# A decoder layer with 32 experts: a fourth load slot, filler products, routing spread over engines, and a write-then-add of the expert sums

## What is computed

```python
logits = (hf @ w_router + b_router).astype(jnp.float32)
top_val, top_idx = lax.top_k(logits, TOP_K)            # TOP_K = 4
gate = jax.nn.softmax(top_val, axis=-1)
...
down = lax.ragged_dot(clamped_swiglu(up), w_down, group_sizes) + b_down[e_sorted]
out = jnp.zeros_like(hf).at[tok].add(down * g_sorted[:, None].astype(down.dtype))
```

## Time and profile before

| what | value |
|---|---|
| time, median of 3 (lowest, highest) | 1441.86 us (1438.42 to 1442.68) |
| the profiled execution's own time | 1445.39 us |
| its span | 1442.3 us |
| TensorE busy | 1299.9 us (90%) |
| VectorE, ScalarE, GpSimd busy | 626.7, 341.7, 313.1 us |
| mean granted clock | 0.978 |
| DMA | 483.70 MB, mean 335 GB/s |

### The profile page before, as it was taken

One profiled execution on the slowest core, in us unless ns is written; L12 is line 12 of the kernel. 1 busy time (PEld: TensorE's weight loads), 2 busy tenths in 40 slices (PEclk: granted clock), 3 DMA queues, 4 the chain that ended last, 5 costly groups with the idle time before them and its releaser, 6 DMA issues.

```text
span 1442.3 us, 45649 instructions
## 1 busy us (share of the span) xinstructions
PE 1299.9 (90%) x18586; PEld 764.2 (53%) x18587; DVE 626.7 (43%) x1667; ACT 341.7 (24%) x860; POOL 313.1 (22%) x423
## 2 busy tenths in 40 slices
PE   5999999999988998988989977899999999998992
PEld 2454555665545555554545534455555555555551
DVE  2467455885573433323333323234334333333335
ACT  2111014774321222211212211122222222221221
POOL 0300002554002222221222211122222222221221
PEclk9999999999999999999999989999999999999996
DMA  9658504003789999999999999999979899999995
GB/s 353 231 206 291 179 12 175 2 2 126 299 334 397 367 396 418 423 427 423 412 423 405 399 425 426 423 418 412 414 322 421 356 370 400 421 425 424 414 419 226
DMA packets 65775, 483.70 MB, mean 335 GB/s; under 512 B 9660, under 2 KB 16612, under 8 KB 45000
## 3 DMA queue, kind: packets, MB, share of 16 engines
q1 hardware_dynamic: 57312, 465.36, 78.0%
q0 software_dynamic: 8144, 17.78, 4.7%
q10 hardware_dynamic: 280, 0.02, 0.0%
HBM read 467.58 MB, written 19.93 MB: 338 GB/s over the span
## 4 chain that ended last, share of the span: by engine, by line
PE 64%; DMA 27%; DVE 5%; issue 2%; ACT 0%; SPq 0%; DVEq 0%; POOL 0%; POOLq 0%; ACTq 0%
PE ps L1953 25%; DMA arena<-in_w_down 23%; PE ps L1973 15%; PE ps L1604 7%; PE ps L1854 4%; PE ps L1719 2%; PE ps L1751 2%; PE ps L1785 2%; DMA arena<-in_w_ada 1%; PE ps L1571 1%; PE ps L1961 1%; DMA arena<-token_numbers 1%; DVE arena L996 1%; DMA arena<-in_w_in 1%; PE ps L1527 1%
## 5 line engine op out<-in xcount | busy, mean ns | idle before, releaser
L1953 PE MATMUL ps<-arena 128*32 128x256 f32 x10240 | 586.8, 383 | 45.6 <-issue 29.4
L1953 PEld LDWEIGHTS ps<-arena 128*32 128x32 f32 x10240 | 343.2, 111 | 266.3 <-issue 57.2
L1973 PE MATMUL ps<-arena 128*32 128x256 f32 x5120 | 302.4, 386 | 40.5 <-DMA arena<-in_w_down 36.2
L1446 DVE TENSOR_SCALAR arena<-ps 128x128 f32<-128x128 f32 x160 | 46.4, 290 | 570.8 <-PE ps L1961 566.2
L1973 PEld LDWEIGHTS ps<-arena 128*32 128x32 f32 x5120 | 155.7, 110 | 164.0 <-issue 45.5
L918 ACT ACTIVATE arena<-ps,arena 32x256 f32<-32x256 f32 x316 | 147.3, 466 | 359.6 <-DMA token_sums<-arena 218.3
L678 POOL DMA_INDIRECT arena<-xn_rows,arena x82 | 85.5, 1043 | 421.9 <-DVE arena L1414 269.3
L670 POOL DMA_INDIRECT token_sums<-arena x80 | 110.4, 1380 | 219.7 <-ACT arena L918 216.7
L909 ACT ACTIVATE arena<-arena 128x128 f32<-128x128 f32 x160 | 49.5, 310 | 416.5 <-DVE arena L1446 416.5
L1604 PE MATMUL ps<-arena 128*128 128x512 f32 (+1 forms) x320 | 129.7, 561 | 2.9 <-DMA arena<-in_w_in 2.9
L653 POOL TENSOR_SCALAR arena<-arena 128x128 f32<-128x128 f32 (+3 forms) x48 | 51.7, 1083 | 204.8 <-DVE arena L1213 193.0
(11 more groups left out here) (339 smaller groups left out, 980.7 us busy)
## 6 DMA issues: line engine op xcount, KB each, us to landing
arena<-in_w_up SPq DMA_DIRECT2D x68, 2048.0 KB, 10.6
arena<-in_w_down SPq DMA_DIRECT2D x64, 2048.0 KB
arena<-in_w_up SPq DMA_DIRECT2D x30, 4096.0 KB
arena<-in_w_ada SPq DMA_DIRECT2D x12, 2048.0 KB, 11.0
arena<-in_w_in SPq DMA_DIRECT2D x5, 2048.0 KB, 9.6
arena<-in_w_o SPq DMA_DIRECT2D x2, 2048.0 KB, 10.9
arena<-in_x SPq DMA_DIRECT2D x4, 512.0 KB, 5.2
arena<-in_w_cmp_v SPq DMA_DIRECT2D x2, 1024.0 KB, 12.5
```

What stands on the lines that cost most here:

```text
L1953: ins = pe.matmul(out_of(y, g), xgT[:, 2 * n + k, :], tiles[par][n][:, k, at:at + 256], start=(n == 0 and k == 0), stop=False)
L1973: ins = pe.matmul(out_of(5, g), actT[:, y, k, :], tiles[par][4 + y][:, k, 256 * g:256 * (g + 1)], start=False, stop=(y == 1 and k == 3))
```

## The change

1. **A fourth load slot.** `ring` gets a fourth buffer. "ada" 8 and 10 go there, and "in" 4 is issued right after "ada" 8, into slot 1, ahead of "ada" 9. The first half of the other compression weight (`wv_half[0]`) and the clearing of `blk`, whose memory the slot overlaps, wait until the row of "ada" 10 is done.
2. **Filler products** of 128 columns: nine before the first modulation product, six before the second, two before tiles 4 and 5 are turned.
3. **Routing.** The gates are normalized before the places are known; GpSimd splits them into three parts and puts a sign on them; the table scaled by token numbers is that of slots (512 columns) and no longer that of chunks (1664); ScalarE copies `picked` and writes `gidx_all`; the gate tables follow after the first rows' transpose. `gate_bits`, `picked` and `tok_chunk` leave the memory of one weight tile, whose load waits no longer for the gates.
4. **Sums.** The sign of a gate tells whether the pair is in the lowest chunk of its token. From it two lists of rows are made. Each chunk issues two scatters: one that writes the rows of tokens met for the first time, one that adds the others. Either list has the other's rows out of bounds. Whoever waited for the one landing waits for both.
5. The last tile's x2 rows are stored after its normed rows.

```diff
-        ring = [take(8192, 4096), take(12288, 4096), take(20480, 4096)]
+        ring = [take(8192, 4096), take(12288, 4096), take(20480, 4096), take(28672, 4096)]
...
-                (("ada", 8), 1), (("ada", 9), 0), (("ada", 10), 1), (("ada", 11), 0), (("in", 4), 1), (("c1", 0), 2),
+                (("ada", 8), 3), (("in", 4), 1), (("ada", 9), 0), (("ada", 10), 3), (("ada", 11), 0), (("c1", 0), 2),
...
-                if (kind, m) == ("ada", 9):
+                if (kind, m) == ("ada", 11):
                     sp.wait_ge(bias_out, 96)
+                    sp.wait_ge(row_sb, ADA_AT[10] + 1)
                     sp.dma_start(wv_half[0], w_c1[1][:, 0:8, :]).then_inc(wv_in, 16)
...
+            idle_products(9)
             pe.wait_ge(silu_ready, 1)
...
             turn_tiles(range(4))
+            idle_products(6)
             ada(2)
             ada_t(0)
             ada_t(2)
+            idle_products(2)
             turn_tiles((4, 5))
...
             def add_rows(c):
                 pool.wait_ge(written, c * 16 + FILLED)
+                pool.wait_ge(placed, c * 16 + FILLED)
                 pool.sem_inc(turn, 1)
+                pool.tensor_copy(idxw, row_first[:, bass.ds(c, 1)]).then_inc(row_idx_moved, 1)
                 pool.tensor_copy(idxs, row_all[:, bass.ds(c, 1)]).then_inc(row_idx_moved, 1)
...
                 pool.wait_ge(y_ready, c + 2)
                 pool.sem_inc(turn, 1)
+                pool.indirect_dma_start(acc_d, bass.IndirectOffsetOnAxis(idxw, 0), ybuf, None,
+                                        bounds_check=SEQ - 1, oob_is_err=False).then_inc(placed, 16)
                 scatter(acc_d, ybuf)
...
             with act_e.Fori(0, total - 1) as c:
                 act_e.wait_ge(tile_used[5], c + 1)
                 act_e.wait_ge(written, c * 16 + FILLED)
+                act_e.wait_ge(placed, c * 16 + FILLED)
...
+            act_e.activation(picked, ps[0:32, 3, 0:NT * MAX_CH].rearrange("p (i c) -> p i c", c=MAX_CH), ACT.Copy)\
+                .then_inc(picked_sb, 1)
+            act_e.wait_ge(spread_ps, 1)
+            act_e.activation(gidx_all, ps[:, 2, 0:MAX_CH], ACT.Identity, scale=-1.0, bias=ck[:, C_QUART:C_QUART + 1])\
+                .then_inc(idx_ready, 1)
...
-            v.tensor_scalar(tok_chunk, in_chunk, const(C_TOK, 1), None, ALU.mult).then_inc(pick_ready, 1)
+            v.tensor_scalar(in_slot_tok, in_slot, const(C_TOK, 1), None, ALU.mult).then_inc(pick_ready, 1)
```

More of the change, by code:

```diff
@@ L206, in hybrid_layer @@
         row_all = take(cur[0] + 8 * MAX_CH, MAX_CH, parts=SLOTS, dt=I32)
+        row_first = take(cur[0], MAX_CH, parts=SLOTS, dt=I32)
+        row_no, first_mark = [take(cur[0] + n * MAX_CH, MAX_CH, parts=SLOTS) for n in (1, 2)]
+        gate_bits = take(cur[0] + 9 * MAX_CH, 24).bitcast(BF16).rearrange("p (m n) -> p m n", n=16)
         ybuf = put(D)[SLOTS:2 * SLOTS, :]
@@ L637, in _ @@
             pool.wait_ge(bias_out, 96)
-            pool.memset(blk[:, :, :, 31:32], 0.0).then_inc(blk_zero, 1)
+            pool.wait_ge(row_sb, ADA_AT[10] + 1)
+            pool.memset(blk[:, :, :, 31:32], 0.0).then_inc(bconst, 1)
             def add_squares(pr):
@@ L1362, in _ @@
             ins.then_inc(order_sb, 1)
+            v.wait_ge(gx_out, 1)
+            link(v.tensor_reduce(gsum, gk, AX.X, ALU.add))
+            link(v.reciprocal(gsum, gsum))
+            v.tensor_tensor(gk, gk, bc(gsum, 2, TOP_K), ALU.mult).then_inc(order_sb, 1)
             v.wait_ge(order_ps, OFF)
@@ L1512, in _, with idle_products @@
             pe.transpose(ps[:, 7, 128:144], cposr, ident[0:16, 0:16]).then_inc(vt_ps, 1)
+            def idle_products(n):
+                for _ in range(n):
+                    pe.matmul(ps[:, 0, 0:P], ident, ident, start=True, stop=True)
+            idle_products(9)
             pe.wait_ge(silu_ready, 1)
@@ L1912, in _, with gate_products @@
                               start=(k == 0), stop=(k == TOP_K - 1))
-            pe.wait_ge(pick_ready, 2)
             for n in range(16):
-                ins = pe.matmul(ps[0:32, 3, 0:MAX_CH], in_slot[:, n, :], tok_chunk[:, n, :], start=(n == 0), stop=(n == 15))
+                ins = pe.matmul(ps[0:32, 3, 0:MAX_CH], in_slot_tok[:, n, :], in_chunk[:, n, :], start=(n == 0), stop=(n == 15))
             ins.then_inc(pick_ps, 1)
-            keep_warm(3)
+            def gate_products(m):
+                pe.wait_ge(gate_ready, m + 1)
+                for n in range(16):
+                    ins = pe.matmul(ps[0:32, 6, 0:MAX_CH], in_slot_gate[m][:, n, :], in_chunk[:, n, :],
+                                    start=(m == 0 and n == 0), stop=(m == 2 and n == 15))
+                return ins
+            gate_products(0)
             pe.wait_ge(picked_sb, 1)
@@ L1923, in _ @@
             ins.then_inc(spread_ps, 1)
-            for m in range(3):
-                pe.wait_ge(gate_ready, m + 1)
-                for n in range(16):
-                    ins = pe.matmul(ps[0:32, 6, 0:MAX_CH], in_slot_gate[m][:, n, :], in_chunk[:, n, :],
-                                    start=(m == 0 and n == 0), stop=(m == 2 and n == 15))
+            gate_products(1)
+            ins = gate_products(2)
             ins.then_inc(gate_ps, 1)
```

116 lines of the change are left out of this document (71 added, 45 removed).

## The result

The changed kernel takes **1449.28 us** (median of 10, 1444.73 to 1455.0), the kernel before beside it 1439.08 (10 runs, 1435.63 to 1446.3): ratio **1.0068, 95% interval 1.0048 to 1.0087**. The profiled execution took 1449.76 us with a span of 1447.7.

What follows compares the result with a forecast made beforehand. Weights and TensorE together were taken to bound the loop. From the profiled 1445.4 us, 7.5 saved before the loop and 15 lost to the second scatter gave 1452.9, or 1449 us on the median's scale; own range 1446 to 1458, 8-in-10 range 1428 to 1468.

Steps and rivals of the forecast that it cites:

- The opening: Ahead of the expert loop: new load order, filler products and routing together save 7.5 us, second gather issued near 427.4 us.
- Fourth slot: Input projection loads: removes TensorE's 2.94 us wait for a piece and the slow 16 products behind it, saving 4.8 us.
- Fillers: Opening's modulation and first projection products: idle products keep TensorE's clock up; gain 1.0 us, bounds 1.3 loss to 2.8 gain.
- Routing: Between gate tables and second gather: smaller scaled table, and work moved to ScalarE and GpSimd, save 1.7 us, bounds 0 and 2.7.
- the reserve: Expert loop: ScalarE's 3.65 us idle before each pair's first sigmoid, which a late landing may use before TensorE's down products wait.
- The other sign of being wrong: Expert loop: the prediction is wrong if TensorE's waits on loading shrink by as much as the new waits grow.
- added landing: Each chunk: the second scatter makes the awaited landing 1.4 to 2.0 us later; lower bound GpSimd's 1.38 us instruction.
- price of the late chunks: TensorE-bound runs of chunks: 12.2 us cycles against 11.3 lose 47 us, less reserve, 11 us; taken as 15 us lost.
- The DMA's own traffic: Indirect queue in the loop: writing instead of adding a quarter of the rows counts 0, bounds 3 us gained and 3 lost.
- (1): Loop rival: later landings fit inside the 3.65 us idle and don't add up, 3 us lost; 1437 us, faster; chance 0.36.
- (3): Loop rival: second scatter queues in full, each landing grows 2.7 us or more, 35 us or more lost; 1470 us; chance 0.08.
- (4): Opening rival: the new order of loads does nothing, something else arrives as late; 4.8 us less gain; chance within the others.

Runs made afterwards that it cites:

- one-scatter kernel: The changed kernel with its fourth slot, filler products and routing, but one adding scatter a chunk as before: 1429.01 us, ratio 0.9922 to the kernel before.
- the empty DMA of 512 B: One adding scatter a chunk plus an indirect DMA of 32 out-of-bounds rows: ahead 1442.14 us, ahead and waited for 1441.18, behind 1427.35, behind and waited for 1444.41.

## Why the prediction was right, point by point

The time was forecast at 1449.0 and came at 1449.28; of the difference, 7.5 us were forecast, and by the ratio it is 9.8. That closeness is partly luck: the rest of the change brought some 3 us more than forecast, with a gain in the tail that no step had, and the scatter's price is 5 us larger; the two partly cancel. Parts are compared below by medians where there are runs, by spans where one execution is read; the profiled execution of before was 3.5 us above the median of its three, that of the one-scatter kernel 3.3 below (1425.73).

**The opening, -7.5 forecast, -7.5 measured** at the second gather (427.41 for 427.4). As a sum it is exact, its parts are not:

```profile
26.93 7.10 PE L1621 MATMUL ps<-arena 128*128 128x512 f32 x16 [0.24 <-DVE arena L1067]
...
427.41 1.10 POOL L693 DMA_INDIRECT arena<-xn_rows,arena  x1 [5.17 <-ACT arena L941]
```

- *Fourth slot*, forecast 4.8: the output projection starts at 341.8 without it and at 336.1 with it, 5.7 us, and 6.1 in the time, give or take 5. The wait that it removes would have been 4.54 us in this kernel, not 2.94, because TensorE arrives earlier at it. Right in mechanism, 1 us small.
- *Fillers*, forecast 1.0 by the clock: next to nothing ahead of the loop (0.2 us). The first 16 projection products are at 7.10 us, as forecast, but without fillers they were too. The Trainium skill (TensorE: Matmul & The Clock Gate, part 1, the HAM clock gate) had said that this varies from run to run; here the trace agrees, 8.80 in one execution and 7.11 in another with the same products ahead. The 1.7 us between these two executions are most of what the parts leave over: slot, fillers and routing measure 5.7, 0.2 and 0.2.
- *Routing*, forecast 1.7: from the output projection's start to the second gather 92.0 us before, 91.8 after. It brought 0.2; in the one-scatter kernel, with the same routing, it is 90.7, 1.3 less than before. The lower bound of the prediction was 0. From the tables' end to the gather it is 5.7 us for 6.1, and the tables come 0.2 later. The sum had 2.7 us for the 44 products behind the tables; they took 3.75, at a granted clock of 0.55. In the one-scatter kernel's execution the clock was full in that stretch (TensorE: length, busy, clock, DMA share, GB/s; first the changed kernel, then that one):

```profile
422.10:425.90 3.80, 3.73 (x45) 0.55 1.02 435
```

```profile
422.10:425.90 3.80, 3.03 (x55) 1.00 1.00 427
```

**The tail, not forecast: -7.3 us.** The last 32 products took from 1415.22 to 1424.53 with their hole, 9.3 us, and 2.0 after. The prediction looked at no row of the tail. That gain nearly hid the next error. A further part of the -13.0 is that the last 32 products begin 12.9 us after the last copy before, and 6.4 after: before, TensorE waited 2.39 us for the last down weights and VectorE 2.49 us for the row of token numbers; in the changed kernel, whose loop ends late, both are there.

**The second scatter, 15 forecast, 20.3 measured.** The mechanism is as forecast: the landing comes later, the reserve is used up (1.3 us left), and TensorE's products wait for ScalarE and VectorE. The prediction's signs: over 65 waits on a landing (71), the first sigmoid under 2 us (1.3), new waits of 15 to 40 us (37.6) all hold, and the landing is later by more than 1 us. The other sign of being wrong came close: TensorE's waits on loading shrank by 31.3 us against the one-scatter kernel while the new waits grew by 36.0. The waits alone leave a loss of some 5 us between these two traces; the rest is busy time of TensorE, which the forecast put at nothing.

- The *added landing*, forecast 1.4 to 2.0 us: 1.36 in the median and 1.20 in the mean (9.92 and 10.20 against 8.56 and 9.00), right at the lower end. The reason given for the lower bound was not right: it took GpSimd's instruction of 1.38, and what stands ahead of the adding scatter is the new one, which is shorter, 0.90 us, plus the gap to the next:

```profile
503.81 0.18 POOL L740 COPY arena<-arena 32x1 int32 x1 [2.81 <-DMA token_sums<-arena]
503.94 0.17 POOL L741 COPY arena<-arena 32x1 int32 x1
506.54 1.01 POOL L746 DMA_INDIRECT token_sums<-arena  x1 [2.42 <-ACT arena L962]
507.86 1.38 POOL L682 DMA_INDIRECT token_sums<-arena  x1 [0.30 <-issue]
...
514.98 0.18 POOL L740 COPY arena<-arena 32x1 int32 x1 [3.06 <-DMA token_sums<-arena]
```

The adding scatter starts 1.3 us behind the writing one in this chunk (1.20 in the median). From its own issue to its landing it takes 7.8 us, alone 7.6, so the delay of the issue is passed on in full, with 0.1 to 0.2 us for what stands in the queue. "About 10 us from the first scatter to the next copy" was 9.37 in the median, and 8.95 before, not 8: the 8.0 of the earlier trace rows was a quick one. The cycle from copy to copy is 12.1 us in the median, as forecast (at least 12.2), and 11.7 in the one-scatter kernel.

- The *price of the late chunks*, forecast 15 us, measured 20.3. The forecast priced a late chunk by its wait alone. What it put at nothing is that TensorE can be slow after a wait. The slowest of the 80 chunks:

```profile
746.43 0.29 PE L2022 MATMUL ps<-arena 128*32 128x256 bf16 x4 [2.12 <-ACT arena L962]
747.60 6.60 PE L2028 MATMUL ps<-arena 128*32 128x256 f32 x64 [0.88 <-DVE arena L1496]
```

This stretch and the one behind it, TensorE's busy time first, then clock and DMA share among the last figures:

```profile
747.60:754.20 6.60, 6.60 (x64) 2.90 (x64) 2.70 (x8) 0.31 (x1) 3.27 (x4) 0.55 0.98 404
754.50:760.00 5.50, 5.50 (x104) 3.49 (x108) 0.00 (x0) 1.88 (x4) 1.81 (x4) 1.00 0.49 157
```

After 2.12 and 0.88 us of idling the 64 down products took 6.60 us, at a granted clock of 0.55, most of it at 1.2 GHz; in an undisturbed chunk they take 3.66 to 3.70. A wait of 3 us cost 6. Over the kernel the down products are busy for 316.4 us against 304.4 in the one-scatter kernel, and TensorE as a whole for 1316.8 against 1295.6: 21 of the 23.8 us between the two spans are busy time, 12 of them the down products. The waits (36.0 us more) are nearly paid by shorter waits on loads (21.8 for 53.1), 5 us net.

This pair of traces overstates it. The changed kernel's profiled execution has the lowest clock of its ten, 0.970, and the one-scatter kernel's the highest of its five, 0.985. Over all executions the means are 0.976 and 0.982; of 1440 us that is 8 us at full speed, an estimate from these clocks. It fits the experiments: 12 to 15 us for a late landing at a nearly unchanged clock (the empty DMA of 512 B), 20 to 27 with the clock lower. The one-scatter kernel's row:

```profile
L2022 PE MATMUL ps<-arena 128*32 128x256 f32 x5120 | 304.4, 388 | 38.5 <-DMA arena<-in_w_down 36.9 <-DVE arena L1490 1.6
```

The Trainium skill (the same page and part) says that the array slows after idling; the prediction used this for the opening and left it out of the loop. Here the trace agrees, with the 6.60 us behind 3 us of idling.

**The DMA's own traffic, 0 forecast:** it holds. The queue's share is 4.5% for 4.7% before, though with 11968 packets for 8144. Rows that are left out are cheap, not absent.

**The rivals.** (1), the reserve takes it, fell. The landing grew by 1.2 to 1.4 us, as it assumed, but the waits added up: it had 3 us lost in all, and the second scatter cost 20.3. (3), queueing in full, fell: a landing longer by 2.7 us on average is nowhere. Both scatters stand in one queue, q0, and there the second passed its later issue on in full. Of the thought that they might share turns and land almost together, which the prediction drew from the Trainium skill's rule for queues (DMA: Bandwidth & Descriptors, queues, rings and completion order), nothing is seen: that rule is on turns between queues. With a reserve of 3.65 us on average, 1.2 to 1.4 us is enough, because the landing spreads by 1.7 us (8.2 to 9.9 between the quartiles before). (4) fell: the order of loads did bring 6 us, give or take 5, and the wait of 2.94 us is gone from the trace.

The best version is the one with a single adding scatter and the rest of the change: 1429 us, faster than both kernels by 10 and 20.

## What to carry to other kernels

A small DMA costs what it adds to the landing that is waited for last. Put it behind that one, unawaited, and it is free; put it ahead or wait for it and even an empty one costs 12 to 15 us over 79 turns with rows of 512 B, and 27 with rows of 4 KB. Price a new wait on TensorE's path with the slow products behind it. And take a change's parts away one by one: the 6.3 us of the filler products were a hole at the other end of the program, which the same 17 products closed from another place too. The row of the instruction queue in that stretch says what such a hole is.

## What was unexpected in the hardware

- An indirect DMA whose rows are all out of bounds still takes packets: 48 a chunk with 32 rows of 4 KB, 32 a chunk with 32 or with 16 rows of 512 B.
- TensorE can stop for 3.5 or 5.5 us amid ready products (line 1993 before) behind a loop. In both kernels that have this hole, and in none of the others, a 16 KB transfer of the instruction queue falls among the last 32 products. 17 more products ahead, in two different places, move the transfer and close the hole.
- Two scatters issued 1.20 us apart from one engine: the second takes 7.8 us from its issue to its landing, alone 7.6. The first, empty or not, hardly slows it; its issue does.
- The kernel with 16 empty rows in place of 32 is 16 us slower at the same landing and a higher clock, with 57.2 us of VectorE's idling laid to no engine. It stays open.
